# Linear recurrence: level one's products taken ahead of the samples' outer products, the states' sum put behind level two's products; attention's constants waited for where they are first used

## The reference, cut to what matters

```python
def gla_chunk(state, inp):            # layer 1, per head; prompt in chunks, samples with one token
    q, k, v, g = inp
    bcum = jnp.cumsum(g, axis=2)
    inter = jnp.einsum('bhtk,bhkv->bhtv', q * jnp.exp(bcum), state)
    diff = jnp.where(causal, bcum[:, :, :, None, :] - bcum[:, :, None, :, :], -jnp.inf)
    att = jnp.einsum('bhtk,bhtsk,bhsk->bhts', q, jnp.exp(diff), k)
    o = inter + jnp.einsum('bhts,bhsv->bhtv', att, v)
    blast = bcum[:, :, -1:, :]
    new_state = jnp.exp(blast)*state + jnp.einsum('bhsk,bhsv->bhkv', k * jnp.exp(blast - bcum), v)
    return new_state, o

# layers 0 and 3: prompt attention under a causal mask, and for the samples
for phys in page_table.T:
    k, v = mla_expand(cache_ckv[la, phys], cache_kpe[la, phys], w_ukv, g_k)
    carry = update(carry, k, v)       # running softmax over the pages, then the new token
```

## Time and profile before

| what | us |
|---|---|
| median of 3 runs (lowest, highest) | 2639.13 (2638.28, 2642.8) |
| the profiled execution: its own time | 2635.24 |
| its span, first to last instruction | 2633.5 |
| TensorE busy in the span | 2288.0 (87%) |
| VectorE, ScalarE, GpSimd busy | 1267.8, 1112.3, 788.3 |

### The profile page before, as it was taken

The page is one execution under the profiler, slowest core; times in us unless marked ns, Lnnn a source line. Parts: engine busy times, 40 slices in busy tenths (PEclk is TensorE's granted clock), DMA queues, the critical chain, the costliest instruction groups (busy, mean ns, idle before and its releaser), DMA issues. The chain is left out here.

```text
span 2633.5 us, 47782 instructions
## 1 busy us (share of the span) xinstructions
PE 2288.0 (87%) x17902; PEld 1904.1 (72%) x17902; DVE 1267.8 (48%) x1958; ACT 1112.3 (42%) x1873; POOL 788.3 (30%) x834
## 2 busy tenths in 40 slices
PE   2999899999758999899976949995979989999987
PEld 1976666666658988888865948995879556666657
DVE  3124455555452666666665154673141445655552
ACT  3036444544333444444443125663221644544531
POOL 4224323222130222222222324543331532322311
PEclk8999999999879999999987979997989989999998
DMA  2210433334213111111103011101012223333432
GB/s 94 69 43 1 125 102 110 110 102 122 97 41 113 42 51 49 35 50 42 42 18 106 24 39 45 46 19 51 16 56 72 76 71 113 111 106 106 114 123 96
DMA packets 102693, 187.60 MB, mean 71 GB/s; under 512 B 15546, under 2 KB 84156, under 8 KB 100692
## 3 DMA queue, kind: packets, MB, share of 16 engines
q1 hardware_dynamic: 102484, 184.81, 22.3%
HBM read 164.84 MB, written 19.92 MB: 70 GB/s over the span
## 5 line engine op out<-in xcount | busy, mean ns | idle before, releaser
L1189 POOL TENSOR_TENSOR latents_t_lo<-pages_t,latents_t_hi 128x256 fp32r<-128x256 f32 x256 | 187.0, 730 | 556.9 <-ACT latents_t_hi L1404 556.0
L380 PE MATMUL ps<-src_hi,w_hi 128*128 128x344 f32 x1008 | 219.0, 327 | 104.0 <-POOL w_lo L351 104.0
L1546 DVE TENSOR_REDUCE sums<-w_uq 128x8 f32<-128x512 f32 x256 | 175.2, 684 | 271.5 <-ACT w_uq L1412 271.0
L1867 PE MATMUL ps<-normed_hi,w_hi 128*128 128x344 f32 x768 | 262.4, 342 | 31.6 <-DMA g_norm<-in_hgrn_g_norm 26.5
L1867 PE MATMUL ps<-normed_lo,w_hi 128*128 128x344 f32 x768 | 252.3, 329 | 0.0
L1867 PE MATMUL ps<-normed_hi,w_lo 128*128 128x344 f32 x768 | 252.1, 328 | 0.0
L380 PEld LDWEIGHTS ps<-src_hi,w_hi 128*128 128x128 f32 x1008 | 173.3, 193 | 106.4 <-POOL w_lo L351 106.4
L1412 ACT ACTIVATE w_uq<-ps 128x512 f32<-128x512 f32 x256 | 152.8, 597 | 213.2 <-PE ps L1266 212.4
L1266 PE MATMUL ps<-w_uk_hi,latents_t_hi 128*128 128x512 f32 x512 | 236.7, 462 | 0.0
L351 POOL TENSOR_TENSOR w_lo<-w_slots,w_hi 128x1024 fp32r<-128x1024 f32 (+1 forms) x50 | 105.1, 2103 | 407.5 <-ACT w_hi L320 407.5
L380 PE MATMUL ps<-src_lo,w_hi 128*128 128x344 f32 x1008 | 217.2, 325 | 0.0
(11 more groups left out here) (303 smaller groups left out, 4906.3 us busy)
## 6 DMA issues: line engine op xcount, KB each, us to landing
pages_t<-in_pages_t SPq DMA_DIRECT2D x256, 208.0 KB, 2.6
pages<-in_pages SPq DMA_DIRECT2D x256, 128.0 KB, 2.1
w_slots<-in_w_hgrn SPq DMA_DIRECT2D x32, 512.0 KB, 3.6
w_slots<-in_w_mla_in SPq DMA_DIRECT2D x18, 512.0 KB, 3.6
x_home<-residual SPq DMA_DIRECT2D x2, 4128.0 KB, 14.8
w_slots<-in_w_rg SPq DMA_DIRECT2D x16, 512.0 KB, 3.4
residual<-in_x SPq DMA_DIRECT2D x4, 1032.0 KB, 7.1
residual<-in_x SPq DMA_DIRECT2D x1, 4128.0 KB, 13.4
```

The lines of the kernel that those rows point to most:

```text
L380: mm = nc.tensor.matmul(c.ps[:, NT * u + t, 0:TT], a[:, u, k, :], b[:, k, cols], start=(k == 0 and n == 0), stop=(k == kt - 1 and n == 2))
L1189: nc.gpsimd.tensor_tensor(lat_lo[:, g % DEPTH, :, :].rearrange("p k t -> p (k t)"), ring[:, g % RING, 0:KVL], lat_hi[:, g % DEPTH, :, :].r ...
L1546: nc.vector.tensor_reduce(ss[:, b % 2, p, :], sq[:, g % 2, :].rearrange("p (h d) -> p h d", h=H), AX.X, ALU.add).then_inc(ssum, 1)
L1867: mm = nc.tensor.matmul(bank[:, 0:TT], w[:, slot, kk, :], x[:, kk, cols], start=(kk == 0 and m == 0), stop=(kk == KD - 1 and m == 2))
```

## The change

In the recurrence, on VectorE, `upper(1)` and `pick(1)` stand right behind `finish` and ahead of the outer products; the loop over the levels skips them. On GpSimd the sum of the states stands behind lower(2) where it stood ahead of it. In attention, the causal mask and `spread` have a semaphore each; TensorE waits for `fold` in `sums` and for `spread` in `spread_inverse`, and no more at its start; VectorE waits for the causal mask alone. No instruction of arithmetic is added or dropped.

```diff
-        p_loads = st.sem("prompt_loads")
+        causal_landed = st.sem("causal_landed")
+        spread_landed = st.sem("spread_landed")
...
-            sp.dma_start(causal[:, :], dram["causal"]).then_inc(p_loads, 16)
+            sp.dma_start(causal[:, :], dram["causal"]).then_inc(causal_landed, 16)
...
-                    sp.dma_start(spread[:, :, :], dram["spread"]).then_inc(p_loads, 16)
+                    sp.dma_start(spread[:, :, :], dram["spread"]).then_inc(spread_landed, 16)
...
                 def sums():
+                    pe.wait_ge(fold_landed, 16)
                     pe.wait_ge(acc_taken, b + 1)
...
             def spread_inverse(G):
                 n = of_tile[G][-1]
+                pe.wait_ge(spread_landed, 16)
...
-            pe.wait_ge(fold_landed, 16)
-            pe.wait_ge(p_loads, 32)
             scores(0, 0)
...
-            dve.wait_ge(p_loads, 32)
+            dve.wait_ge(causal_landed, 16)
             row_max(0, 0)
...
                 for l in range(LEVELS):
-                    if l == 2:
-
-                        pool.wait_ge(outer, 2 * h + 2)
-                        pool.wait_ge(sin_scaled, h + 1)
-                        nc.gpsimd.tensor_tensor(ns[:, :, :], ns[:, :, :], sin[:, :, :], ALU.add) \
-                          .then_inc(ns_done, 1)
                     half = P >> (l + 1)
                     pool.wait_ge(exped, 17 * h + (2 * l + 2))
...
                                             halves(k[:, 0:SEQ], half)[:, :, 0, :], ALU.mult).then_inc(zp_done, 1)
+                    if l == 2:
+
+                        pool.wait_ge(outer, 2 * h + 2)
+                        pool.wait_ge(sin_scaled, h + 1)
+                        nc.gpsimd.tensor_tensor(ns[:, :, :], ns[:, :, :], sin[:, :, :], ALU.add) \
+                          .then_inc(ns_done, 1)
...
                     finish(h - 1, 1 - u)
+                dve.wait_ge(scanned, 8 * h + 2)
+                upper(1)
+                pick(1)
                 dve.wait_ge(k_done, h + 1)
...
-                    dve.wait_ge(scanned, 8 * h + (l + 1))
-                    upper(l)
-                    pick(l)
+                    if l > 1:
+                        dve.wait_ge(scanned, 8 * h + (l + 1))
+                        upper(l)
+                        pick(l)
```

## The result

The changed kernel takes 2597.11 us in the median (2596.15 to 2599.4, 4 runs), against 2638.7 for the kernel before beside it: a ratio of 0.9841, 95% interval 0.9824 to 0.9858. That is 41.6 us less; 2597 was predicted. Its profiled execution took 2596.15 us with a span of 2594.4, where before's was 2633.5: 39.1 us less.

The account below looks back on a forecast made before the run. TensorE, the busiest engine, was taken to stand still for VectorE's upper products and at attention's start. Terms -37.4 + 2.4 - 1.2 - 6.3 = -42.5 from 2635.2 give 2592.7; with 3.9 for the median, 2597 us, range 2586 to 2616.

Parts of the forecast that it names:

- Level one: Recurrence, head 2: with upper(1) issued earlier, TensorE idles 0.85 us ahead of level one for 5.43.
- Level two: Recurrence, head 2: a new TensorE wait of 0.75 us ahead of level two, where there was none.
- Level three: Recurrence, head 2: TensorE idles 1.35 us ahead of level three for 0.91, with weight_lo held up by the moved sum.
- The stretches: Broadcasts' end to level three's start, heads 0 to 6: 12.35 us each, 86.45 against 123.85 in all, -37.4 us.
- The moved sum gives back some: Recurrence, level three: without the moved sum it would start at TensorE's own 1011.85 instead of 1013.2.
- Clock in the heads: Recurrence stretches: heads 1, 4 and 6 keep a fall to 1.2 GHz, 0.8 us each, +2.4 us.
- The last head: Recurrence's last head, without filling units, paced by VectorE and GpSimd: -1.2 us, bounds 0 and 5.4 us.
- Attention: Start of both attention stages: page one starts 3.16 us earlier, 2.3 to 4.0 by the clock; -6.3 us for both.
- The wait did not form again: Rival, recurrence: GpSimd's sum, weight_lo and difference(4) collide worse or exponentials come late; 15.5 us a stretch, 2617 us; chance 0.18.
- Slower by the clock: Rival, recurrence: three short gaps keep 1.2 GHz from broadcasts to level three in every head; +6, 2645 us; chance 0.03.
- Attention alone: Rival: the heads give nothing, level one's products come no earlier, only attention's 6.3 us is left; 2633 us; chance 0.05.
- no change: Rival, whole kernel: the stall isn't where the time goes; 2639 us; chance 0.02.

Follow-up runs that it names:

- GpSimd's part alone: The changed kernel with upper(1) and pick(1) put back in VectorE's loop, behind the outer products and difference(2); 2621.89 us, ratio 0.9929.
- VectorE's part alone: The changed kernel with GpSimd's sum of the states put back between lower(1) and lower(2); 2603.86 us, ratio 0.9865.
- sum last: The changed kernel with GpSimd's sum of the states behind lower(4) instead of lower(2); 2594.76 us, ratio 0.9824.
- weight later: The changed kernel with weight_lo of the third weight moved on VectorE from behind pick(2) to behind pick(3); 2590.38 us, ratio 0.9814.
- heads only: The changed kernel with the attention part undone, so only the recurrence is changed; 2601.15 us, ratio 0.9859.
- after again: The changed kernel unaltered, run again as the measure for group two; 2597.52 us, ratio 0.9837.
- attention only: The changed kernel with the recurrence as before and the rest of the change kept; 2634.51 us, ratio 0.9978.
- before again: The kernel before, unaltered, one more profiled execution for two more attentions with the old start; 2642.05 us.

## Why the prediction was right, point by point

- **Level one.** Predicted idle 0.85 us for 5.43; 0.84 in head 2. That the sum made upper(1) late was the heart of the argument, and GpSimd's part alone shows it: 0.68 us for upper(1), level one 2.15 us earlier with VectorE's order as before.
- **Level two.** A new wait of 0.75 predicted, 0.59 found. Level three: 1.35 predicted, 1.45 found, by the row of turns that was laid out (`weight_lo` to 995.51, 1.08 behind the sum, was predicted as 1.1 behind it). The stretches: 86.45 us predicted, 88.85 with the clock's 2.4; 85.45 found, 87.05 in the second profile of after. The chain laid out the turns of pairs right; the same reckoning for VectorE's part alone missed two turns and was off by 11 us.
- **"The moved sum gives back some"** is right on level three, which in sum last waits 0.25 us for 1.45 in head 2; weight later shows that `weight_lo` was the link that could go. That the outer products keep their length "beside whatever GpSimd did" can't be read from the earlier trace rows, where the sum starts behind them; the picks show it (below).
- **Clock in the heads.** +2.4 us for three heads was too much. In after the clock fell in four, heads 3 to 6, some 0.3 to 1.0 us behind the broadcasts; in head 4 the stretch of lowered clock is this window:

```profile
1125.47:1128.88 3.41, 3.41 (x41) 3.35 (x40) 3.41 (x5) 1.15 (x2) 0.00 (x0) 0.50 0.02 5
```

  It is 3.41 us long for the 10.24 of the earlier trace rows. Heads 1 and 2 are at 12.30 and 12.27 us without a fall in after, at 12.66 and 12.62 with one in heads only: 0.36 us each, since levels two and three wait less in exchange. Four of them are 1.4 us. A longer fall costs more: head 2 of after again, with the clock down for 6.8 us, takes 13.73. The Trainium skill (TensorE: Matmul & The Clock Gate, section Why this matters for your kernels) would let gaps of about one microsecond pass. Here heads 3 to 6 fell with gaps of 0.10 to 0.86 us, and heads 1 and 2, with 0.86 and 0.84, did not: gaps alone don't decide it.
- **The last head.** -1.2 predicted; from its level zero to its last matmul it takes 50.5 us for 50.7. Level one starts 5.4 us earlier there, and levels two and three then wait 4.54 and 3.93 us where they waited 1.86 and 2.53.
- **Attention.** 3.16 us a start predicted, 3.1 and 2.9 found, with 5.17 us idle ahead of page one for about 5.5. What reaches the end is 1.4 and 1.3 us between the two profiles, and 5.8 for both by the runs of attention only (3.4 to 8.2), whose interval holds the 6.3. The prediction left 0.85 us either way for the clock at the start; the clock acted some 410 us later, behind the pages, and for 3.4 us more or less of 1.2 GHz. (A sixth of 5.58 is 0.93, and level two's 1006.35 should be 1006.25; nothing hangs on either.)
- **The sum.** -42.5 predicted, -41.6 between the medians, -39.1 between the two profiled executions. Of the 3.4 us between, 3.0 lie in a part that the change does not touch, from the recurrence's end to the second attention: 716.7 us in the profile of before, 719.7 in that of after, and 719.7 in that of before again. The profiled execution of before was a quick one there, and the 3.9 us that the prediction put between it and the median were its distance, not that of a usual execution (after's profile lies 1.0 below its median). So the order of the work was right, and the size of the terms nearly, but 2597 to the microsecond is luck: the stretches with the clock came out 3.4 us better than laid out, the last head, attention and the untouched part 7.6 worse between the profiles, and the 3.9 covered the rest.
- **The rivals.** The wait did not form again: 12.2 us a stretch, not 15.5. Slower by the clock: with three short gaps the clock was down for 3.4 us in four heads of seven, at some 0.36 us each; the half clock that this rival feared, in every head, is in GpSimd's part alone, with one gap of 3.28 us. Attention alone and no change are out by the 41.6 us and by upper(1)'s 0.68.

## What to carry to other kernels

When a two-input instruction lasts several times its usual length, look for one on the other of VectorE and GpSimd that overlaps it, and move the one that nobody needs soon; then lay the whole row out again, because each instruction behind it meets a new neighbour. Of a row of work ahead of a late matmul, ask of each link when its own user needs it: moving `weight_lo`, whose own user came 5 us behind level three, brought 7.1 us, and moving the sum again brought nothing that the runs can show. Count a saved wait as idle time, and treat what a stage keeps of it as uncertain by the clock: here 3.4 us of idle time a stage came out as 1.3 between two profiles and as 2.9 (1.7 to 4.1) over the runs.

## What the runs showed of the hardware

- **Turns, not shares.** A two-input VectorE instruction on 128x1024 issued while GpSimd's ran ended 1.08 us behind GpSimd's end in four places (2.41, 2.30, 3.32 us long, and `difference(3)` in VectorE's part alone), one on 128x512 0.54 or 0.55 behind it, however early it was issued. Lower(3) behind `weight_lo` did the same from the other side, 1.14. The Trainium skill (SBUF — State Buffer, section Who interferes with whom) calls the ports that the two engines share an exclusive lock, has a VectorE instruction with two inputs in SBUF contend with a GpSimd instruction that reads SBUF, and takes those with at most one, outside the 2-port modes, as free of it. The trace agrees on both: pick(2), whose data comes from PSUM and only its mask from SBUF, kept 1.30 us (990.85) with lower(2) beside it to 992.07.
- **A stage's clock has a habit.** Six attention stages with after's start lay within 0.4 us of each other in three profiles, while six with the old start scattered over 4.3 us, all by TensorE's busy time. The fall behind the pages makes the difference. Ahead of it TensorE waits 1.57, 1.16 and 0.62 us in before, in after and in heads only's second stage alike; then the clock went down for 3.4 us, for 6.8 and not at all. Why it differs stays open.
